# Two-block transformer layer on one core: order of the value units, the odd probabilities and the last gate's tanh

## The chip, the core and the metric

The kernel runs on one core of a Trainium2 chip. A core has TensorE (PE, matmuls into PSUM), VectorE (DVE), ScalarE (ACT), GpSimd (POOL) and SyncE (SP, which here only issues DMAs). The engines run side by side, each through its own list of instructions in order, and wait for one another on semaphores. The metric is the time of one execution on the device, in microseconds.

## The reference, cut to what matters

The reference is two blocks one after the other, on one sequence of 256 tokens and 1024 channels. The change touches only the second, and of it only the part ahead of the experts:

```python
h = rms_norm_2(x, norm1_g[l])
proj = h @ w_in[l]
q, ckv, qi, ki, wi, u, v, ga, gb = jnp.split(proj, splits, axis=-1)
...
q_lat = jnp.einsum('bthd,rhd->bthr', q, w_uk[l])
o_lat = sparse_attention(q_lat, q_idx, w_idx, c_kv, ki, rel_bias)
o_a = jnp.einsum('bthr,rhd->bthd', o_lat, w_uv[l]).reshape(B, T, ATTN_WIDTH)
y_a = o_a @ w_proj_a[l]
y_b = chunked_gmlp(u, v, ln_v_g[l], ln_v_b[l], w_spatial[l], b_spatial[l]) @ w_proj_b[l]
merged = jax.nn.sigmoid(ga) * y_a + jax.nn.sigmoid(gb) * y_b
x = x + merged @ w_out[l]
h2 = rms_norm_2(x, norm2_g[l]).reshape(B * T, D)
y = hier_moe(h2, ...)
```

In `sparse_attention` an index score (queries `qi`, keys `ki`, relu, weighted by `wi`) picks 64 keys for each token; the attention's softmax runs over these, in the latent space `c_kv`. `chunked_gmlp` takes the gelu of `u` and `v`, a layer norm of `v`, mixes the tokens of each chunk of 128 by `w_spatial`, and multiplies by `u`. `hier_moe` is 32 experts, of which each token uses two.

## The kernel before

Everything is float32. A product is made of three matmuls: weights and activations are each split into a high part (`w_hi`, `xT_hi`) and a low part (`w_lo`, `xT_lo`), and `mm3` (L1790 to L1794) adds low by high, high by low and high by high.

The projection of the second block runs in **units** of 256 columns, `w` = 0 to 16. For each unit SyncE loads 1 MB of weights into one of four `raw` slots, ScalarE copies the high part (`hi2`, the activation at L737, possible once TensorE is done with unit `w - 2`), VectorE subtracts to get the low part (`split2`, L1154), and TensorE multiplies, 48 matmuls in two halves, into one of three PSUM banks. In unit `w`'s turn ScalarE and VectorE make the halves of unit `w + 2`. Then ScalarE evacuates the bank of unit `w`. The order of the units stands in a table (L80): `W_QI` 0 and 1 are index queries, `W_K` 2 the keys, `W_Q` 3 and 4 the queries, `W_V` 5 and 6 the gating values v, `W_U` 8 and 9 the gating u, the rest are gates. Columns of w_in_2 are loaded to match.

What depends on the results is woven into the units, by hand, at fixed numbers. On each engine a function `small(w, half)` holds the pieces for half a unit; TensorE runs `small(w, 0)` between the halves of unit `w` and `small(w, 1)` behind them.

- `X_IX` = 4: eight index scores in units 4 to 7 (TensorE L2103, relu on ScalarE L959, weighted sums on VectorE L1465 and L1467). They need the turned keys, which ScalarE copies at the end of its turn 3 (L1015 and L1016).
- `TOP_AT`: VectorE finds the top keys in six parts, at the end of its turns 5, 6, 7 (first 128 tokens) and 9, 10, 11 (the others), by MAX8 and MATCH_REPLACE. The last part of each gives the mask that GpSimd adds to the bias of the scores (L698).
- `GELU_AT`: a gelu unit is evacuated by a square and a copy (L1001, L1002), VectorE's polynomial (L1501, after its split), ScalarE's tanh (L1004), VectorE's product (L1518, after top keys and layer norm if there are any).
- `X_LNV` = 8: in this turn VectorE takes the layer norm's statistics of the value half (L1505 to L1512), behind its split; a turn later ScalarE normalises (L1020), and then GpSimd multiplies by the gain and adds the bias (L688, L690).
- `X_QL` = 8: the queries go to the latent space (L2113).
- `X_SP` = 10: behind unit 10, TensorE mixes the tokens (L2166, waits for GpSimd), and VectorE multiplies by u (L1525). `X_YB` = 11: behind units 11 and 12 the result is turned (L2175), ScalarE takes its high part and VectorE, as the last piece of turns 11 and 12, its low part (`yb_lo`, L1530). The second turning waits for the first `yb_lo`, and the first output matmul of the attention (L473) for the second, since all use one PSUM bank.
- `X_S` = 11: eight attention tasks, two a unit, in units 11 to 14. VectorE adds the bias and takes the maximum (L1481, L1482), ScalarE the exponential (L973), VectorE normalises (`probabilities`, L1452 and L1453), TensorE turns the result two half-units after the scores (L454), then values and output. Before, `small` normalises task s - 1 right ahead of the scores of task s, so that the odd ones come in the turn after their own.

At the end of the units ScalarE's turn 16 holds the high half of unit 18, then the tanh of the last gate (L1007), for which the first unit of the projection (17) waits (`ev2`). Then come the projections, `w_out`, the router and the experts, whose weights (96 MB) stream through a ring of seven tiles that are refilled as TensorE frees them.

Of the kernel before, what the change touches and what calls it, by code (L numbers as in the profile page):

```python
# [58 lines left out]
UCOLS = 2048  # L59
# [19 lines left out]
G2 = LAYERS * UNITS  # L79
W_QI, W_K, W_Q, W_V, W_U, W_PB, W_PA, W_OUT, W_R = 0, 2, 3, 5, 8, 17, 19, 21, 25  # L80
GELU_AT = (W_V, W_V + 1, W_U, W_U + 1)
# [14 lines left out]

X_IX, X_QL, X_LNV, X_SP, X_YB, X_S = 4, 8, 8, 10, 11, 11

# [24 lines left out]
def build(nc, t, out):  # L123
    ctx = ExitStack()
    with ctx:
# [376 lines left out]
        def _(sp):  # L502
# [79 lines left out]
            col_of.update({w: O_GA + 256 * g for g, w in enumerate(GATE_AT)})  # L582
            for w in range(W_Q, W_PB):
                load2(w, w2[:, :, col_of[w]:col_of[w] + 256], KC, 256)
# [138 lines left out]
        def _(act):  # L723
# [252 lines left out]
            for w in range(W_PB):  # L976
                small(w, 0)
                exponentials(w, 0)
                small(w, 1)
                hi2(G2 + w + 2, W_COLS.get(w + 2, UCOLS))  # L980
                exponentials(w, 1)
# [3 lines left out]
                if w == W_K:  # L985
# [6 lines left out]
                    nc.scalar.activation(wi[:], rows[:, :, P + HD:K_COLS], ACT.Copy, scale=IDX_SCALE).then_inc(ev2, 1)  # L992
                elif w < W_Q:
                    nc.scalar.activation(qiT[:, 2 * (w - W_QI):2 * (w - W_QI) + 2, :], two, ACT.Copy).then_inc(ev2, 1)
                elif w < W_V:
                    nc.scalar.activation(q2T[:, 2 * (w - W_Q):2 * (w - W_Q) + 2, :], two, ACT.Copy).then_inc(ev2, 1)
                elif w in GELU_AT:
                    n = GELU_AT.index(w)
                    if n >= 1:
                        act.wait_ge(gel_out, n)  # L1000
                    nc.scalar.activation(gel_s, bank, ACT.Square)  # L1001
                    nc.scalar.activation(gel_x, bank, ACT.Copy, scale=0.5).then_inc(ev2, 1)  # L1002
                    act.wait_ge(gel_poly, n + 1)
                    nc.scalar.activation(gel_s, gel_s, ACT.Tanh, scale=2.0 * GELU_C * 0.044715).then_inc(gel_th, 1)  # L1004
                else:
                    g = 2 * GATE_AT.index(w)
                    nc.scalar.activation(gT[:, g:g + 2, :], two, ACT.Tanh, scale=0.5).then_inc(ev2, 1)  # L1007
# [14 lines left out]
                if w in (X_YB, X_YB + 1):  # L1022
                    r = w - X_YB
                    act.wait_ge(ybT_done, r + 1)
                    nc.scalar.activation(br_hi[:, 1, 2 * r:2 * r + 2, :], ps[:, TB, :].rearrange("p (c t) -> p c t", c=2), ACT.Copy).then_inc(yb_hi, 1)
            for w in range(W_PB, W_OUT):
                hi2(G2 + w + 2, W_COLS.get(w + 2, UCOLS))
                if w >= W_PA:
                    j = w - W_PA
                    act.wait_ge(proj_a, j + 1)  # L1030
                    nc.scalar.activation(xT_hi[:, 4 * j:4 * j + 4, :], gT[:, 4 * j:4 * j + 4, :], ACT.Copy, scale=0.5).then_inc(pm_hi, 1)
# [86 lines left out]
        def _(dve):  # L1118
# [278 lines left out]
            def split2(u, n=UCOLS, i=None):  # L1397
                split(0, u, n, None if i is None else i * 12)
# [56 lines left out]
            def small(w, half):  # L1455
# [15 lines left out]
                s = latent_task(w, half)  # L1471
                if s is not None and s >= 1:
                    probabilities(s - 1)
                if s is not None:
# [7 lines left out]
                    nc.vector.tensor_reduce(nm2[:, s % 4, :], e, AX.X, ALU.max, negate=True).then_inc(s2_max, 1)  # L1482
                if (w, half) == (X_S + 4, 0):
                    probabilities(7)

            for w in range(W_PB):
# [9 lines left out]
                small(w, 1)  # L1496
                split2(G2 + w + 2, W_COLS.get(w + 2, UCOLS))
                if w in GELU_AT:
                    n = GELU_AT.index(w)
# [922 lines left out]
```

## Time and profile before

| | us |
|---|---|
| median of 3 runs | 1373.38 |
| lowest, highest | 1372.72, 1373.8 |
| the profiled execution | 1373.0 |
| its span | 1371.2 |
| TensorE busy | 1290.9 (94%) |
| VectorE busy | 905.2 (66%) |
| ScalarE busy | 586.7 (43%) |
| GpSimd busy | 59.8 (4%) |

The profile is of one execution. Times in it count from the start of the span. A timeline lists the instructions of an engine with their start and length; a number in brackets is the idle time ahead of one and what ended it. An instruction's length covers its whole way through the engine, so that the next one can start a little before its end; a step from start to start is the better measure of cost. A view of stretches gives the busy time of each engine, and the clock that was granted to TensorE, as a share of its full 2.4 GHz. The first block ends at about 913 us, the units of the second run from 922 to 1066, the experts from 1134.

### The profile page before, as it was taken

The page shows a single profiled execution, that of the slowest core. Times are in us where ns is not written, and L with a number is a line of the kernel's source. Part 1 is how long each engine was busy: PE and PEld are TensorE (multiplying, and loading weights), DVE is VectorE, ACT ScalarE, POOL GpSimd, SP SyncE. Part 2 cuts the span into 40 slices and gives each one's busy share as a digit, 9 for nine tenths or more (in the row PEclk, how much of TensorE's full clock was granted, in tenths as well). Part 3 has the DMA queues.
Part 4 walks back from the last instruction along what each step waited for, and adds up shares of the span by engine and source line. Part 5 has one row for each costly group of instructions (what it writes and reads, how often), then busy time and mean ns, then how long its engine had stood idle before and what let it go on. Part 6 is the DMA issues. An engine that isn't in the chain of part 4 may idle for free.

```text
span 1371.2 us, 21689 instructions
## 1 busy us (share of the span) xinstructions
PE 1290.9 (94%) x8713; PEld 1093.8 (80%) x8713; DVE 905.2 (66%) x1464; ACT 586.7 (43%) x911; POOL 59.8 (4%) x84
## 2 busy tenths in 40 slices
PE   7999999999999899999998999969979979999996
PEld 6999999788888799989987888859879866555553
DVE  3999877875555789997687555584885672223223
ACT  3345675434444334566544444444535343111111
POOL 1000000000000000000000000020043000011000
PEclk9999999999999999999999999989989989999998
DMA  9754435465555456443456555555535586999994
GB/s 282 244 196 152 156 93 155 153 215 184 188 193 198 128 184 218 137 154 101 148 183 207 192 184 184 184 172 158 155 111 187 205 303 257 419 420 421 420 421 191
DMA packets 172583, 289.70 MB, mean 211 GB/s; under 512 B 10388, under 2 KB 143140, under 8 KB 160204
## 3 DMA queue, kind: packets, MB, share of 16 engines
q1 hardware_dynamic: 169580, 281.55, 58.6%
q0 software_dynamic: 2752, 6.82, 1.7%
q8 instruction: 62, 1.02, 0.3%
q14 instruction: 29, 0.24, 0.0%
q10 hardware_dynamic: 160, 0.08, 0.0%
HBM read 287.36 MB, written 3.16 MB: 212 GB/s over the span
## 4 chain that ended last, share of the span: by engine, by line
PE 61%; DVE 25%; ACT 5%; DMA 5%; issue 3%; POOL 0%; SPq 0%; DVEq 0%; ACTq 0%; POOLq 0%
PE ps L1792 11%; PE ps L1794 10%; PE ps L1793 10%; DVE w_lo L1154 8%; PE ps L1843 8%; PE ps L2289 7%; DVE cvh L1277 5%; ACT w_hi L737 4%; PE ps L1845 4%; PE ps L2321 3%; DMA raw<-in_w_up 2%; DMA w_exp<-in_w_up 2%; PE ps L2332 2%; DVE nm L1234 1%; DVE gT L1194 1%
## 5 line engine op out<-in xcount | busy, mean ns | idle before, releaser
L1154 DVE TENSOR_TENSOR w_lo<-raw,w_hi 128x2048 fp32r<-128x2048 f32 (+1 forms) x165 | 369.6, 2240 | 147.4 <-ACT w_hi L737 147.2
L737 ACT ACTIVATE w_hi<-raw 128x2048 fp32r<-128x2048 f32 (+1 forms) x165 | 307.4, 1863 | 233.1 <-PE ps L1794 218.4
L1792 PE MATMUL ps<-xT_both,w_lo 128*128 128x256 f32 x680 | 198.1, 291 | 0.0
L1793 PE MATMUL ps<-xT_both,w_hi 128*128 128x256 f32 x680 | 193.3, 284 | 0.0
L1794 PE MATMUL ps<-xT_both,w_hi 128*128 128x256 f32 x680 | 193.0, 284 | 0.0
L1843 PE MATMUL ps<-xT_both,w_hi 128*128 128x512 f32 x496 | 176.0, 400 | 0.0
L1792 PE MATMUL ps<-w_hi,xT_both 128*128 128x256 f32 (+2 forms) x536 | 161.9, 302 | 1.9 <-DVE w_lo L1154 1.7
L1793 PE MATMUL ps<-w_lo,xT_both 128*128 128x256 f32 (+2 forms) x536 | 159.1, 297 | 0.0
L1794 PE MATMUL ps<-w_hi,xT_both 128*128 128x256 f32 (+2 forms) x536 | 159.1, 297 | 0.0
L1792 PEld LDWEIGHTS ps<-xT_both,w_lo 128*128 128x128 f32 x680 | 131.4, 193 | 3.0 <-issue 2.7
L1793 PEld LDWEIGHTS ps<-xT_both,w_hi 128*128 128x128 f32 x680 | 131.3, 193 | 0.2
L1794 PEld LDWEIGHTS ps<-xT_both,w_hi 128*128 128x128 f32 x680 | 131.1, 193 | 0.0
L1845 PE MATMUL ps<-xT_both,w_lo 128*128 128x256 f32 x434 | 121.6, 280 | 0.0
L1792 PEld LDWEIGHTS ps<-w_hi,xT_both 128*128 128x128 f32 x536 | 102.4, 191 | 8.4 <-issue 2.9
L1843 PEld LDWEIGHTS ps<-xT_both,w_hi 128*128 128x128 f32 x496 | 90.8, 188 | 22.3 <-issue 5.3
L1794 PEld LDWEIGHTS ps<-w_hi,xT_both 128*128 128x128 f32 x536 | 102.3, 191 | 2.9
L1793 PEld LDWEIGHTS ps<-w_lo,xT_both 128*128 128x128 f32 x536 | 102.4, 191 | 2.6
L1277 DVE SCALAR_TENSOR_TENSOR cvh<-cvh,prm 128x256 f32<-128x256 f32 x240 | 98.3, 479 | 0.1
L1726 DVE TENSOR_TENSOR xT_both<-ps,xT_both 128x512 fp32r<-128x512 f32 x32 | 22.1, 692 | 113.5 <-ACT xT_both L1106 113.5
L1792 PE MATMUL ps<-w_hi,br_lo 128*128 128x512 f32 x240 | 93.7, 391 | 0.3 <-DVE br_lo L1353 0.3
L1794 PE MATMUL ps<-w_hi,br_hi 128*128 128x512 f32 x240 | 93.4, 389 | 0.0
L1793 PE MATMUL ps<-w_lo,br_hi 128*128 128x512 f32 x240 | 93.4, 389 | 0.0
(410 smaller groups left out, 2264.6 us busy)
## 6 DMA issues: line engine op xcount, KB each, us to landing
raw<-in_w_in SPq DMA_DIRECT2D x72, 1024.0 KB, 5.1
raw<-in_w_ff SPq DMA_DIRECT2D x64, 1024.0 KB, 5.3
raw<-in_w_down SPq DMA_DIRECT2D x10, 1024.0 KB, 16.0
raw<-in_w_up SPq DMA_DIRECT2D x10, 1024.0 KB, 17.5
w_exp<-in_w_down SPq DMA_DIRECT2D x10, 1024.0 KB, 17.6
raw<-in_w_o SPq DMA_DIRECT2D x8, 1024.0 KB, 4.9
w_exp<-in_w_gate SPq DMA_DIRECT2D x8, 1024.0 KB, 16.9
raw<-in_w_gate SPq DMA_DIRECT2D x8, 1024.0 KB, 17.7
```

Source lines behind the costliest of these rows:

```text
L737: nc.scalar.activation(split_of(u)[0][:, 0:n], raw[:, u % RAW, 0:n], ACT.Copy).then_inc(hi_done, 1)
L1154: nc.vector.tensor_tensor(split_of(u)[1][:, 0:n], raw[:, u % RAW, 0:n], split_of(u)[0][:, 0:n].bitcast(F32), ALU.subtract).then_inc(split_ ...
L1277: nc.vector.scalar_tensor_tensor(out=cv[:, c, :], in0=hpad[:, c, k:k + T], scalar=w, in1=cv[:, c, :], op0=ALU.mult, op1=ALU.add).then_inc( ...
L1726: nc.vector.tensor_tensor(y_lo[h], ps[:, Y_BANKS[h], :], y_hi[h].bitcast(F32), ALU.subtract).then_inc(y_lod[h], 1)
L1792: nc.tensor.matmul(out_, left[1], right[0], start=start, stop=False)
L1793: nc.tensor.matmul(out_, left[0], right[1], start=False, stop=False)
L1794: return nc.tensor.matmul(out_, left[0], right[0], start=False, stop=stop)
L1843: last = nc.tensor.matmul(both, w_c[0][:, k, :], xT_both[:, k].rearrange("p i t -> p (i t)"), start=k == 0, stop=k == KC - 1)
L1845: nc.tensor.matmul(high, w_c[1][:, k, :], xT_hi[:, k, :], start=False, stop=False)
L2289: last = nc.tensor.matmul(gate_up(r, p)[s, kind * T:(kind + 1) * T], x, duos[duo_slot(r, d)][e][:, k * T:(k + 1) * T], start=k == 0, stop= ...
L2321: last = nc.tensor.matmul(ps[s, Y_BANKS[h], :], heT[:, c, s], duos[duo_slot(r, d)][e][:, c * D + h * BANK:c * D + (h + 1) * BANK], start=c ...
L2332: last = nc.tensor.matmul(ps[:, ACC + 2 * a + h, :], place[p % PLACES][:, a, :], y, start=p == 0 and k == 0, stop=p == PAIRS - 1 and k == 1)
```

## The change

Three things, all in the second block:

1. The table of units: the value units are now 3 and 4, the query units 5 and 6, and `X_LNV` is 5. The loads and the evacuations follow. `X_QL`, `X_IX`, `TOP_AT` and `X_SP` stay.
2. VectorE's `small` normalises task s - 1 only in the second half of a unit, which are the even tasks; the odd ones are normalised behind the split of their own turn, ahead of the top keys.
3. On ScalarE the high half of unit 18 comes behind the last gate's tanh.

```diff
--- before.py
+++ after.py
@@ -77,7 +77,7 @@
 O_Q, O_KV, O_QI, O_KI, O_WI, O_U, O_V, O_GA, O_GB = (int(c) for c in np.cumsum((0, 512, 128, 512, 64, 8, 512, 512, 1024)))
 
 G2 = LAYERS * UNITS
-W_QI, W_K, W_Q, W_V, W_U, W_PB, W_PA, W_OUT, W_R = 0, 2, 3, 5, 8, 17, 19, 21, 25
+W_QI, W_K, W_V, W_Q, W_U, W_PB, W_PA, W_OUT, W_R = 0, 2, 3, 5, 8, 17, 19, 21, 25
 GELU_AT = (W_V, W_V + 1, W_U, W_U + 1)
 GATE_AT = (7, 10, 11, 12, 13, 14, 15, 16)
 TOP_AT = {5: (0, 0), 6: (0, 1), 7: (0, 2), 9: (1, 0), 10: (1, 1), 11: (1, 2)}
@@ -94,7 +94,7 @@
 PLACES = 3
 PROJ_BANKS = ((5, 6), (7, 4))
 
-X_IX, X_QL, X_LNV, X_SP, X_YB, X_S = 4, 8, 8, 10, 11, 11
+X_IX, X_QL, X_LNV, X_SP, X_YB, X_S = 4, 8, 5, 10, 11, 11
 
 
 def raw_inc(u):
@@ -580,7 +580,7 @@
             col_of = {W_Q + j: O_Q + 256 * j for j in range(2)}
             col_of.update({w: o for w, o in zip(GELU_AT, (O_V, O_V + 256, O_U, O_U + 256))})
             col_of.update({w: O_GA + 256 * g for g, w in enumerate(GATE_AT)})
-            for w in range(W_Q, W_PB):
+            for w in range(W_K + 1, W_PB):
                 load2(w, w2[:, :, col_of[w]:col_of[w] + 256], KC, 256)
             for w0, name in ((W_PB, "w_proj_b_2"), (W_PA, "w_proj_a_2")):
                 for j in range(2):
@@ -977,7 +977,8 @@
                 small(w, 0)
                 exponentials(w, 0)
                 small(w, 1)
-                hi2(G2 + w + 2, W_COLS.get(w + 2, UCOLS))
+                if w < W_PB - 1:
+                    hi2(G2 + w + 2, W_COLS.get(w + 2, UCOLS))
                 exponentials(w, 1)
                 bank = ps[:, UB + w % 3, :]
                 two = bank.rearrange("p (c t) -> p c t", c=2)
@@ -990,9 +991,9 @@
                     for i in range(2):
                         nc.scalar.activation(ki2[:, :, i, :], rows[:, :, P:P + HD], ACT.Copy)
                     nc.scalar.activation(wi[:], rows[:, :, P + HD:K_COLS], ACT.Copy, scale=IDX_SCALE).then_inc(ev2, 1)
-                elif w < W_Q:
+                elif w in (W_QI, W_QI + 1):
                     nc.scalar.activation(qiT[:, 2 * (w - W_QI):2 * (w - W_QI) + 2, :], two, ACT.Copy).then_inc(ev2, 1)
-                elif w < W_V:
+                elif w in (W_Q, W_Q + 1):
                     nc.scalar.activation(q2T[:, 2 * (w - W_Q):2 * (w - W_Q) + 2, :], two, ACT.Copy).then_inc(ev2, 1)
                 elif w in GELU_AT:
                     n = GELU_AT.index(w)
@@ -1023,6 +1024,7 @@
                     r = w - X_YB
                     act.wait_ge(ybT_done, r + 1)
                     nc.scalar.activation(br_hi[:, 1, 2 * r:2 * r + 2, :], ps[:, TB, :].rearrange("p (c t) -> p c t", c=2), ACT.Copy).then_inc(yb_hi, 1)
+            hi2(G2 + W_PB + 1)
             for w in range(W_PB, W_OUT):
                 hi2(G2 + w + 2, W_COLS.get(w + 2, UCOLS))
                 if w >= W_PA:
@@ -1469,7 +1471,7 @@
                 for kind, s in latent_steps(w, half):
                     latent_dve(dve, kind, s)
                 s = latent_task(w, half)
-                if s is not None and s >= 1:
+                if s is not None and half == 1:
                     probabilities(s - 1)
                 if s is not None:
                     nk = P * (s // 4 + 1)
@@ -1480,8 +1482,6 @@
                         dve.wait_ge(t2_done, s - 3)
                     then(nc.vector.tensor_tensor(e, ps[:, s % 2, :].rearrange("p (i k) -> p i k", i=2)[:, :, 0:nk], bias_t[:, s % 2, :, 0:nk], ALU.add))
                     nc.vector.tensor_reduce(nm2[:, s % 4, :], e, AX.X, ALU.max, negate=True).then_inc(s2_max, 1)
-                if (w, half) == (X_S + 4, 0):
-                    probabilities(7)
 
             for w in range(W_PB):
                 if w == W_K + 1:
@@ -1495,6 +1495,8 @@
                 small(w, 0)
                 small(w, 1)
                 split2(G2 + w + 2, W_COLS.get(w + 2, UCOLS))
+                if latent_task(w, 1) is not None:
+                    probabilities(latent_task(w, 1))
                 if w in GELU_AT:
                     n = GELU_AT.index(w)
                     dve.wait_ge(ev2, w + 1)

```

In the changed kernel lines move by one (from ScalarE's gate on) or two (VectorE and after).

**ScalarE, from the high half made in turn 3 on.** `gT` is the gelu's working space, `cvh` the turned keys, `qkT` the queries. Before:

```order
L737 ACTIVATE w_hi<-raw 128x2048
L996 ACTIVATE qkT<-ps 128x512
L1015 ACTIVATE cvh<-ps 128x256
L1016 ACTIVATE cvh<-ps 128x256
L959 ACTIVATE wide<-ps 128x2x128 x2
```

After:

```order
L737 ACTIVATE w_hi<-raw 128x2048
L1002 ACTIVATE gT<-ps 128x512
L1003 ACTIVATE gT<-ps 128x512
L1005 ACTIVATE gT<-gT 128x512
L1016 ACTIVATE cvh<-ps 128x256
L1017 ACTIVATE cvh<-ps 128x256
L959 ACTIVATE wide<-ps 128x2x128 x2
```

One copy ahead of the turned keys has become three activations, the last of which waits for VectorE.

**VectorE, turn 5 and the start of turn 6.** The L1424 group is the first top keys, L1465 to L1468 the index sums, L1154 the split. Before (ahead of it the split of turn 5):

```order
L1501 SCALAR_TENSOR_TENSOR gT<-gT 128x512
L1424 TENSOR_TENSOR wide<-wide,mask 128x128
L1425 MAX nw<-wide 128x8
...
L1518 SCALAR_TENSOR_TENSOR vv<-gT 128x2x256
L1465 TENSOR_SCALAR wide<-wide,wi 128x256
L1467 SCALAR_TENSOR_TENSOR wide<-wide,wi 128x256
L1468 MEMSET nw 128x1
L1467 SCALAR_TENSOR_TENSOR wide<-wide,wi 128x256 x2
L1468 MEMSET nw 128x1
L1154 TENSOR_TENSOR w_lo<-raw,w_hi 128x2048
```

After, from the split of turn 5 (L1156), layer norm (L1507 to L1514), top keys (L1426 on), index sums, split of turn 6:

```order
L1156 TENSOR_TENSOR w_lo<-raw,w_hi 128x2048
L1507 BN_STATS st<-vv 128x6 x2
...
L1514 SCALAR_TENSOR_TENSOR nmr<-mv,nw 128x2
L1426 TENSOR_TENSOR wide<-wide,mask 128x128
L1427 MAX nw<-wide 128x8
...
L1467 TENSOR_SCALAR wide<-wide,wi 128x256
L1469 SCALAR_TENSOR_TENSOR wide<-wide,wi 128x256
L1470 MEMSET nw 128x1
L1469 SCALAR_TENSOR_TENSOR wide<-wide,wi 128x256 x2
L1470 MEMSET nw 128x1
L1156 TENSOR_TENSOR w_lo<-raw,w_hi 128x2048
```

The layer norm now stands ahead of the top keys of turn 5, and index sums and the split of unit 8's weights follow them; the gelu's polynomial and product are gone from here.

**VectorE, turn 11, from its split to the next score.** L1452 and L1453 normalise task 1, L1432 begins the last top keys, L1443 ends them, L1530 is `yb_lo`. Before:

```order
L1154 TENSOR_TENSOR w_lo<-raw,w_hi 128x2048
L1432 MAX nw<-cvh 128x8
...
L1443 TENSOR_TENSOR cvh<-cvh,mask 128x128
L1530 TENSOR_TENSOR br_lo<-ps,br_hi 128x512
L1452 RECIPROCAL rs<-rs 128x2
L1453 TENSOR_TENSOR qkT<-qkT,rs 128x2x128
```

After:

```order
L1156 TENSOR_TENSOR w_lo<-raw,w_hi 128x2048
L1454 RECIPROCAL rs<-rs 128x2
L1455 TENSOR_TENSOR qkT<-qkT,rs 128x2x128
L1434 MAX nw<-cvh 128x8
...
L1445 TENSOR_TENSOR cvh<-cvh,mask 128x128
L1532 TENSOR_TENSOR br_lo<-ps,br_hi 128x512
```

The two normalising instructions have moved from behind the top keys and `yb_lo` to ahead of them.

**ScalarE, turn 16.** L1007 is the last gate's tanh, L737 the high halves. Before:

```order
L489 ACTIVATE cvh<-ps 128x256
L492 ACTIVATE br_hi<-ps 128x128 x2
L737 ACTIVATE w_hi<-raw 128x2048
L1007 ACTIVATE gT<-ps 128x512
L737 ACTIVATE w_hi<-raw 128x2048 x3
```

After:

```order
L489 ACTIVATE cvh<-ps 128x256
L492 ACTIVATE br_hi<-ps 128x128 x2
L1008 ACTIVATE gT<-ps 128x512
L737 ACTIVATE w_hi<-raw 128x2048 x4
```

The tanh now stands ahead of the high half, which joins the three that follow.

## Rows read from the trace of the kernel before

**Rows 1.** Timeline of TensorE: start, length (us), engine, line, tiles, [idle before, releaser].
```profile
1004.40 3.78 PE L2166 MATMUL ps<-vv,rot 128*128 128x128 f32 x16 [6.75 <-POOL vv L690]
...
1024.81 0.44 PE L454 MATMUL ps<-ident,qkT 128*128 128x128 f32 x2 [2.69 <-DVE qkT L1453]
...
1031.86 0.44 PE L473 MATMUL ps<-cvh,gT 128*64 128x128 f32 x4 [0.23 <-DVE br_lo L1530]
...
1068.93 0.36 PE L1792 MATMUL ps<-br_hi,w_lo 128*128 128x256 f32 x1 [2.71 <-ACT gT L1007]
```

**Rows 2.** Timelines of VectorE, ScalarE, TensorE: unit 3's end, a polynomial, a tanh.
```profile
948.48 2.29 DVE L1154 TENSOR_TENSOR w_lo<-raw,w_hi 128x2048 fp32r<-128x2048 f32 x1 [0.78 <-ACT w_hi L737]
...
949.09 0.39 ACT L1016 ACTIVATE cvh<-ps 128x256 f32<-128x256 f32 x1
...
951.22 0.49 PE L2103 MATMUL ps<-cvh,qkT 64*128 64x128 f32 x4
...
966.60 0.68 DVE L1501 SCALAR_TENSOR_TENSOR gT<-gT 128x512 f32<-128x512 f32 x1
...
967.32 0.63 ACT L1004 ACTIVATE gT<-gT 128x512 f32<-128x512 f32 x1 [1.99 <-DVE gT L1501]
```

**Rows 3.** Timelines of VectorE (top keys, index sums, layer norm) and TensorE (unit 8's start).
```profile
967.21 0.28 DVE L1424 TENSOR_TENSOR wide<-wide,mask 128x128 f32<-128x128 f32 x1
...
970.40 0.69 DVE L1518 SCALAR_TENSOR_TENSOR vv<-gT 128x512 f32<-128x512 f32 x1
...
971.01 0.35 DVE L1465 TENSOR_SCALAR wide<-wide,wi 128x256 f32<-128x256 f32 x1
...
972.97 2.29 DVE L1154 TENSOR_TENSOR w_lo<-raw,w_hi 128x2048 fp32r<-128x2048 f32 x1
...
989.60 1.28 DVE L1505 BATCH_NORM_STATS2 st<-vv 128x6 f32<-128x512 f32 x2
...
993.45 0.68 DVE L1518 SCALAR_TENSOR_TENSOR vv<-gT 128x512 f32<-128x512 f32 x1
...
976.84 0.39 PE L1792 MATMUL ps<-w_hi,xT_both 128*128 128x256 f32 x1
```

**Rows 4.** Timelines of ScalarE, GpSimd and VectorE around the two multiplies.
```profile
971.86 0.58 ACT L1001 ACTIVATE gT<-ps 128x512 f32<-128x512 f32 x1
...
997.66 1.50 ACT L1020 ACTIVATE vv<-vv,nmr,nw 128x512 f32<-128x512 f32 x2
...
999.25 2.35 POOL L688 TENSOR_TENSOR vv<-vv,wide 128x1024 f32<-128x1024 f32 x1 [72.18 <-ACT vv L1020]
...
1001.68 2.67 POOL L690 TENSOR_TENSOR vv<-vv,wide 128x1024 f32<-128x1024 f32 x1
...
1000.28 0.43 DVE L1429 MAX8 nw<-cvh 128x8 f32<-128x256 f32 x1
...
1002.08 4.42 DVE L1154 TENSOR_TENSOR w_lo<-raw,w_hi 128x2048 fp32r<-128x2048 f32 x1
```

**Rows 5.** Stretches, TensorE alone: from:to, length, PE busy, granted clock, DMA share, GB/s.
```profile
1009.00:1010.00 1.00, 1.00 (x10) 0.93 1.07 382
...
1029.00:1030.00 1.00, 1.00 (x8) 0.69 0.00 0
```

**Rows 6.** Timeline of VectorE from the last products on.
```profile
1012.01 0.42 DVE L1481 TENSOR_TENSOR qkT<-ps,wide 128x256 f32<-128x256 f32 x1 [0.48 <-PE ps L2126]
...
1014.03 0.93 DVE L1453 TENSOR_TENSOR qkT<-qkT,rs 128x256 f32<-128x256 f32 x1
...
1015.32 0.42 DVE L1481 TENSOR_TENSOR qkT<-ps,wide 128x256 f32<-128x256 f32 x1 [0.36 <-PE ps L2126]
...
1016.89 2.60 DVE L1154 TENSOR_TENSOR w_lo<-raw,w_hi 128x2048 fp32r<-128x2048 f32 x1 [0.69 <-ACT w_hi L737]
```

**Rows 7.** Timeline of ScalarE, the weight half ahead of the last tanh.
```profile
1066.44 1.90 ACT L737 ACTIVATE w_hi<-raw 128x2048 fp32r<-128x2048 f32 x1
```

**Rows 8.** Stretches, all engines: busy us of each, PEclk, DMA share, GB/s.
```profile
1200.00:1250.00 50.00, 50.00 (x344) 27.82 (x341) 13.79 (x27) 7.56 (x16) 4.73 (x8) 1.00 1.01 421
```

## The prediction

> **What bounds the kernel now.** I read the timeline of the tensor engine first, and in it the rows that carry an idle time. Between the end of the first block and the experts it waits long at four places only [rows 1]: 6.75 us for GpSimd's second multiply on the value half (ahead of the spatial matmuls), 2.69 us for the odd probabilities of task 1, 0.23 us for VectorE's low half of the second turned branch (`yb_lo`), 2.71 us for the tanh of the last gate. The change aims at the first, second and fourth. The third looks harmless, and is what to watch: it says that at 1031.86 VectorE, not TensorE, set the pace. From the row of the last products (L1525) on, VectorE's own chain (scores, exponentials, splits, top keys) runs up to that point almost without a pause [rows 6]. What TensorE gains ahead of 1031.86 is therefore worth only what VectorE's chain gains with it.
>
> The experts follow everything. There the DMA engines are full (share 1.01, 421 GB/s, [rows 8]) and refill a ring of tiles that TensorE frees, so whatever TensorE's start there moves by, the end moves by, one for one.
>
> The sum is made against the profiled execution, 1373.0 us (span 1371.2 and 1.8 around it), which lies 0.4 under the median of the three runs, 1373.38. About 0.2% (2.7 us) is what a measurement of this kernel can tell from no change.
>
> **Part 1: value units at 3 and 4.** The same matmuls, the same splits; what moves is who waits.
>
> (a) Unit 3's evacuation on ScalarE was one copy; now it is square, copy, a wait for VectorE's polynomial, tanh, and only then the copies of the turned keys, for which the first index score waits. VectorE can give the polynomial after the split that starts at 948.48, which takes 2.2 us until the next instruction can start: 950.7. From polynomial to tanh is 0.72 us (966.60 to 967.32), the tanh takes 0.54 to its successor (its row lists 0.63 of busy time), so the key copies start at 951.95 and end 0.65 later at 952.60, where they ended at 949.48; with 0.1 us of handing over TensorE goes on at 952.70. It came for the first index score at 951.22 [rows 2]. Cost **+1.5 us**, and TensorE is the pace from there to unit 7.
>
> (b) The layer norm's statistics leave unit 8's turn of VectorE, where it had room, for unit 5's, right ahead of the first top keys. At unit 5 VectorE was through with its split at 966.60 [rows 2], now at 968.08. Behind that in program order: layer norm 3.85 us (989.60 to 993.45), top keys 3.19 (967.21 to 970.40), the two index sums of unit 6 1.96 (971.01 to 972.97), then the split of unit 8's weights, 2.29. That gives 979.37. TensorE began unit 8 at 976.84 and would be ready for it at 978.3 [rows 3]. So even undisturbed it waits 1.1 us.
>
> (c) It is not undisturbed. GpSimd's two multiplies come as soon as ScalarE has normalised. ScalarE began unit 5's evacuation at 971.86 for the split behind it; the same place, now at unit 6, is 973.3, plus 0.5 for the copy of the queries, plus 1.5 for the two normalising activations: 975.3. GpSimd runs from 975.4, and at 975.1 VectorE has just left the top keys for the index sums. In the trace the split that met the second multiply took 4.42 us instead of 2.29, while a MAX8 inside the first took its 0.43 [rows 4]. So top keys pass, splits and sums with two operands wait, about 2.1 us for each multiply (4.42 less 2.29). SyncE's load of unit 12 follows the same split and so comes 7 us late too; it has three units' turns as cover. Four index-sum instructions and the split stand there, so that both multiplies find one to hold: 979.37 plus 4.2 is 983.6. TensorE waits **5.3 us** and starts unit 8 6.8 us later than before (1.5 of it is (a)).
>
> The page Advanced Engine Details and Errata of the Trainium skill (VectorE Performance Modes) says that GpSimd's instructions and VectorE's two-port ones block each other, and VectorE: DVE Perf Modes (Why tensor_tensor can't do 2×_2P) that a tensor_tensor is never one of these. By these two together the split would run free and at most the first index sum be held. The trace disagrees: the held split is a tensor_tensor with both operands in SBUF. By the pages the time would be that of rival B below, by the row that of this sum.
>
> (d) After such a wait the clock of TensorE is granted low. After the 6.75 us wait it was at its lower level, 1.2 GHz, for 4.7 us (1004.4 to 1009.1), and after the 2.69 us wait for 3.3 us (1026.4 to 1029.7), though that one came 1.6 us after the restart [rows 1, 5]. Half of such a time is lost: 2.35 and 1.6 at most. The wait here lies between; I take 2.2 as nearer to the long one. TensorE and all that hangs on its unit ends is then **9.0 us** late at unit 9, and with it the split of unit 11, from which VectorE works without a pause to the last products.
>
> (e) What is won: the 4.42 us split becomes 2.29, **-2.1**. The 6.75 us wait goes, but only for TensorE: it arrives 3 us early at the turning of the branch and waits there for the same products. The last products end 9.0 - 2.1 = +6.9 late.
>
> **Part 2: odd probabilities.** No instruction is added; each odd normalisation stands one place earlier. The chain from the last products to `yb_lo` of unit 12 changes so: two idle times of VectorE fall away because TensorE and ScalarE are ready early, 0.48 and 0.69, -1.2, and a wait of 0.36 for TensorE's scores, -0.3. Task 1's stood in this chain before too, so moving it is free, save that it now meets GpSimd's bias add (as task 0's did: 0.93 against the 0.42 of an add of the same size, [rows 6]), +0.5. Task 3's stood behind `yb_lo` and now stands ahead of it: some 0.6 for its two instructions (0.93 less the 0.5, and a small reciprocal) and up to 1.0 us behind GpSimd's 512-wide add (half of what the 1024-wide multiply holds), +1.6. Sum **+0.6**. Tasks 5 and 7 are free: VectorE idles there. The 2.69 us wait goes, but TensorE then waits longer at `yb_lo`. It resumes 6.9 + 0.6 = **7.5 us** late at the place of 1031.86.
>
> (f) That wait is again 3 us or more, so a low clock behind it: as after the 2.69 us wait, +1.6 at most. But before, half of unit 13 was slow too and ended at this very point, so part is no news; between 0 and 2.4 I take **+1.6**, by the row of the 2.69 us wait.
>
> **Part 3: the last tanh.** Its row starts 0.1 behind the end of a weight half that starts at 1066.44 and takes 1.90; now the tanh starts at 1066.44. TensorE waits 0.9 instead of 2.71: **-1.8**. The weight half, 0.6 later, has unit 17's 5.8 us of matmuls as cover; without that cover it would cost 0.6 [rows 1, 7].
>
> Sum: 7.5 + 1.6 - 1.8 = +7.3, 1373.0 + 7.3 = **1380.3 us**. Bounds of the clock terms: (d) 1.6 to 2.4, (f) 0 to 2.4, so 1378.1 to 1381.3. If only one of the two multiplies holds VectorE up, 2.1 less and a shorter slow clock (0.6 less), 1377.6.
>
> **Rivals.**
> A. The forecast, slower. For it: four instructions in program order, each with its row.
> B. GpSimd doesn't hold the index sums and the split (they fall beside top keys, or pass). Then TensorE waits 1.1 at unit 8 with no clock lost: 1.5 + 1.1 = +2.6, -2.1, +0.6, -1.8, clock 0 to +1.6: -0.7 to +0.9, 1372.3 to 1373.9, no change. It decides with the start of the multiplies: if they begin before 973, top keys cover most of them.
> C. Faster: VectorE keeps up. If the tanh and the layer norm cost no wait at units 4 and 8 (because ScalarE reaches the key copies in time and some row above is shorter there), what is left is -2.1 + 0.6 - 1.8 = -3.3, and 0 to 1.6 of clock: 1369.7 to 1371.3. It needs the split of unit 8 before 976.9, 2.5 us under the undisturbed chain of (b). That the three waits just vanish (6.75 + 2.69 + 1.8 = 11.2 us less, 1361.8) I exclude: two of them stand ahead of a wait for VectorE.
>
> **How the numbers follow.** A 0.62 (1378.1 to 1381.3 by its clock bounds), one multiply only 0.10 (about 1377.6), B 0.18, C 0.10. C gives faster 0.10 (its upper end, 1371.3, is just not faster; its chance is kept whole because a shorter clock loss is as likely there); the rest of B and a little of the single multiply give same 0.20; slower 0.70. The range takes in B and A's bounds and the upper half of C, 1370.0 to 1383.0; above A it leaves 1.7 us for a third low clock, behind the wait at the first turning of the branch, which the sum has at nothing because VectorE's chain covers it.
>
> **What would show it.** In the timeline after: an idle of 1.5 us ahead of the first index score (A, B); ahead of unit 8 one of 5 us released by VectorE's split (A), of 1 us (B), none (C); no wait ahead of the spatial matmuls; instead waits of about 3 us at both turnings of the branch and at the first output matmul, released by L1525's and L1530's successors; the tanh wait at 0.9. VectorE's index-sum rows at unit 6 with 2 us more each would confirm the block. I am wrong if TensorE's wait ahead of unit 8 is under 2 us, or if the waits at the turnings are short.

## The result and the profile after

| | us |
|---|---|
| changed kernel, median of 5 runs | 1378.41 (1376.98 to 1379.61) |
| before, on the same chip, median of 5 | 1373.38 (1372.16 to 1373.80) |
| ratio, 95% interval | 1.0036 (1.0024 to 1.0047) |
| profiled execution, its span | 1379.22, 1377.4 |
| TensorE, VectorE, GpSimd busy | 1292.9, 908.2, 57.2 |

Slower by 5.0 us, as forecast: 1380.3 was 1.9 too high. The profiled execution is 6.2 above that of before, of which the sum had said 7.3. The work is the same (TensorE's busy time differs by 2 us); what differs is who waits. The timeline of TensorE in the changed kernel, the rows with an idle time between unit 3 and the last gate, in the order of [rows 1] (start, length, engine, line, tiles, [idle before, releaser]):

```profile
947.48 0.33 PE L2159 MATMUL ps<-ident,cvh 128*128 128x128 f32 x1 [1.32 <-DVE cvh L1493]
952.36 0.49 PE L2105 MATMUL ps<-cvh,qkT 64*128 64x128 f32 x4 [1.35 <-ACT cvh L1017]
983.15 0.58 PE L1794 MATMUL ps<-w_hi,xT_both 128*128 128x256 f32 x1 [5.09 <-DVE w_lo L1156]
1017.84 0.66 PE L2177 MATMUL ps<-ident,vv 128*128 128x128 f32 x4 [3.16 <-DVE vv L1527]
1029.37 0.63 PE L2177 MATMUL ps<-ident,vv 128*128 128x128 f32 x4 [1.87 <-DVE br_lo L1532]
1037.74 0.69 PE L473 MATMUL ps<-cvh,gT 128*64 128x128 f32 x4 [4.21 <-DVE br_lo L1532]
1075.38 0.36 PE L1794 MATMUL ps<-br_hi,w_lo 128*128 128x256 f32 x1 [0.91 <-ACT gT L1008]
```

The three long waits of before are gone or short: none ahead of the spatial matmuls (6.75), none for the probabilities (2.69), 0.91 for the tanh (2.71) [rows 1]. The first row stood before too. Of the others the last is what is left of the 2.71; the five between (1.35, 5.09, 3.16, 1.87, 4.21) are new or longer, and VectorE releases four of them. The one of 5.09 ahead of unit 8 is the new thing. VectorE and GpSimd just ahead of it (timelines of both, same columns):

```profile
974.84 0.35 DVE L1467 TENSOR_SCALAR wide<-wide,wi 128x256 f32<-128x256 f32 x1
975.23 5.02 DVE L1469 SCALAR_TENSOR_TENSOR wide<-wide,wi 128x256 f32<-128x256 f32 x2
980.28 0.48 DVE L1469 SCALAR_TENSOR_TENSOR wide<-wide,wi 128x256 f32<-128x256 f32 x1
980.81 2.29 DVE L1156 TENSOR_TENSOR w_lo<-raw,w_hi 128x2048 fp32r<-128x2048 f32 x1
...
975.09 2.40 POOL L688 TENSOR_TENSOR vv<-vv,wide 128x1024 f32<-128x1024 f32 x1 [48.28 <-ACT vv L1021]
977.57 2.40 POOL L690 TENSOR_TENSOR vv<-vv,wide 128x1024 f32<-128x1024 f32 x1
```

Two index-sum instructions take 5.02 us together; they end at 980.25, 0.3 after GpSimd's second pass (977.57 + 2.40 = 979.97). The split behind them, which TensorE waits for, is undisturbed at 2.29 but starts at 980.81, where before it started at 972.97 [rows 3].

To compare executions I count from the matmul of unit 3 at 947.48 (before: 947.76), the last place that the change doesn't touch; it comes between 945.87 (part 1 alone) and 948.32 (parts 2 and 3) in the profiled executions, though what runs up to there is the same work in all of them. The table gives the distance from there to the first output matmul (L473, before at 1031.86) and to the one that waits for the last gate (before at 1068.93), in the profiled execution of each kernel, and the medians of the timed runs against those of before on the same chip. All experiments, which follow, are in it.

| kernel | wait ahead of unit 8 | to L473 | to last gate | against before | median (before) |
|---|---|---|---|---|---|
| before | 0 | 84.10 | 121.17 | | |
| changed | 5.09 | 90.26 | 127.90 | +6.73 | 1378.41 (1373.38) |
| part 1 alone | 5.08 | 88.24 | 125.32 | +4.15 | 1377.92 (1373.53) |
| part 2 alone | 0 | 85.37 | 122.44 | +1.27 | 1376.23 (1373.53) |
| part 3 alone | 0 | 83.75 | 119.03 | -2.14 | 1370.06 (1373.53) |
| parts 2 and 3 | 0 | 85.38 | 120.65 | -0.52 | 1371.24 (1373.82) |
| changed, key copies first | 5.09 | 87.95 | 124.77 | +3.60 | 1374.74 (1373.53) |
| changed, top keys later | 0 | 82.99 | 118.27 | -2.90 | 1371.49 (1373.91) |
| changed, tiny multiplies | 1.09 | 84.22 | 121.06 | -0.11 | 1372.49 (1373.91) |
| changed, task 3 late | 5.09 | 88.50 | 126.58 | +5.41 | 1378.10 (1373.91) |
| the three edits together | 0 | 80.16 | 115.43 | -5.74 | 1368.37 (1373.91) |
| the same without part 2 | 0 | 79.83 | 115.10 | -6.07 | 1367.52 (1373.82) |

What one execution's distance and what the medians say of an edit differ by up to 2.4 us (key copies first: +3.60 and +1.2). Part of that goes with the granted clock, as the section on what was not expected shows.

### The profile page after: what moved, and what is told of

Its sections match the earlier page's. It is cut to its first block, busy times and chain, and to the rows that moved or that the text cites. A ratio compares the mean times of both kernels' runs of the same rounds, so it can differ in the third digit from the quotient of the medians.

```text
span 1377.4 us, 21689 instructions
## 1 busy us (share of the span) xinstructions
PE 1292.9 (94%) x8713; PEld 1095.4 (80%) x8713; DVE 908.2 (66%) x1464; ACT 586.7 (43%) x911; POOL 57.2 (4%) x84
## 3 DMA queue, kind: packets, MB, share of 16 engines
HBM read 287.36 MB, written 3.16 MB: 211 GB/s over the span
## 4 chain that ended last, share of the span: by engine, by line
PE 61%; DVE 27%; ACT 5%; DMA 3%; issue 3%; SPq 1%; DVEq 0%; ACTq 0%
PE ps L1794 10%; PE ps L1796 10%; PE ps L1795 10%; DVE w_lo L1156 9%; PE ps L1845 8%; PE ps L2291 7%; DVE cvh L1279 5%; ACT w_hi L737 4%; PE ps L1847 3%; PE ps L2323 3%; DMA raw<-in_w_up 2%; PE ps L2334 2%; DVE nm L1236 1%; DVE gT L1196 1%; DVE x_nat L1202 1%
## 5 line engine op out<-in xcount | busy, mean ns | idle before, releaser
L1156 DVE TENSOR_TENSOR w_lo<-raw,w_hi 128x2048 fp32r<-128x2048 f32 (+1 forms) x165 | 367.1, 2225 | 152.2 <-ACT w_hi L737 152.1
L737 ACT ACTIVATE w_hi<-raw 128x2048 fp32r<-128x2048 f32 (+1 forms) x165 | 307.4, 1863 | 230.3 <-PE ps L1796 215.4
```

What stands on the lines that cost most here:

```text
L737: nc.scalar.activation(split_of(u)[0][:, 0:n], raw[:, u % RAW, 0:n], ACT.Copy).then_inc(hi_done, 1)
L1156: nc.vector.tensor_tensor(split_of(u)[1][:, 0:n], raw[:, u % RAW, 0:n], split_of(u)[0][:, 0:n].bitcast(F32), ALU.subtract).then_inc(split_ ...
```

## Experiments

### The three parts, each by itself

Each is the diff's own lines of that part (`W_V`, `W_Q`, `X_LNV` and the loads; `probabilities`; `hi2` of unit 18), with the others as before.

**Part 1 alone.** 

> Part 1 alone (value units at 3 and 4, layer norm in turn 5); odd probabilities and last tanh as before. The theory of the prediction: part 1 carries the whole loss. The wait of 5.1 us ahead of unit 8 stays as in the changed kernel (which hangs on nothing of parts 2 and 3), the wait for the last tanh is 2.7 again instead of 0.9 (+1.8), and what part 2 gave back in the chain to the first output matmul (measured -0.3) is missing. About 1378.4 + 1.8 + 0.3 = 1380.5, +7 over before. Rival (part 2 is what costs, through the normalisation ahead of yb_lo): then this kernel stands at or under before, 1371 to 1374, with no wait ahead of unit 8.

Measured: 1377.92, ratio 1.0037 (1.0024 to 1.0050), 4.4 slower. The wait ahead of unit 8 is 5.08, so it belongs to part 1 and needs nothing of the others. The rival falls. But the expectation of +7 was too high: the first output matmul is only 4.14 late (88.24 - 84.10), 2.0 less than in the changed kernel. So part 2 takes 2.0 us there, where I had taken it to give back 0.3. TensorE's wait and VectorE's rows with part 1 alone:

```profile
981.55 0.58 PE L1792 MATMUL ps<-w_hi,xT_both 128*128 128x256 f32 x1 [5.08 <-DVE w_lo L1154]
...
1015.69 0.41 DVE L1481 TENSOR_TENSOR qkT<-ps,wide 128x256 f32<-128x256 f32 x1
...
1018.55 0.41 DVE L1481 TENSOR_TENSOR qkT<-ps,wide 128x256 f32<-128x256 f32 x1
...
1019.33 2.28 DVE L1154 TENSOR_TENSOR w_lo<-raw,w_hi 128x2048 fp32r<-128x2048 f32 x1
```

The three idle times of [rows 6] (0.48, 0.36, 0.69) are gone and the split takes 2.28, not 2.60, without part 2. Once part 1 has made VectorE late, TensorE and ScalarE are ready for it. I had booked this gain to part 2.

**Part 2 alone.** 

> Odd probabilities alone, on the kernel before. The theory: the 2.69 us wait ahead of 1024.81 goes, and TensorE waits instead for yb_lo at the place of 1031.86, because VectorE's chain from the last products to yb_lo is hardly shorter. The 0.48 of idle time goes, the normalisation of task 3 now stands ahead of yb_lo (+1.3 by its row in the changed kernel): -1 to +1.5 us, 1372.4 to 1374.9, that is no change. Rival (the waits of TensorE simply add up): the 2.69 us and the low clock behind it go, 1373.4 - 2.7 - 1.6 = 1369.1.

Measured: 1376.23, ratio 1.0020 (1.0009 to 1.0030), slower by 2.7. The rival, in which the waits of TensorE add up to a gain, is out, and my own range was too low by 1.3. In the trace the 2.69 is gone and TensorE waits for `br_lo` twice:

```profile
1024.20 0.72 PE L2175 MATMUL ps<-ident,vv 128*128 128x128 f32 x4 [1.99 <-DVE br_lo L1530]
1032.56 0.44 PE L473 MATMUL ps<-cvh,gT 128*64 128x128 f32 x4 [2.68 <-DVE br_lo L1530]
1069.63 0.55 PE L1792 MATMUL ps<-br_hi,w_lo 128*128 128x256 f32 x1 [2.71 <-ACT gT L1007]
```

By distance it loses 1.27, within what was expected. The rest came later, behind the last gate's wait: from there to the end of the span are 305.4 us, before 302.3. Parts 2 and 3 together, below, are the test of that.

**Part 3 alone.** 

> Last tanh ahead of the weight half alone, on the kernel before. The theory: TensorE's wait there falls from 2.71 to 0.9 us, and since nothing behind it waits for another engine, the end moves by the same 1.8: 1373.4 - 1.8 = 1371.6. Rival (the stream of weights sets the end, not TensorE's start): no change, 1373.4, with the wait gone all the same.

Measured: 1370.06, ratio 0.9974 (0.9963 to 0.9984), 3.5 faster. The wait is 0.91 as forecast, and the end follows TensorE's start: the rival falls. The gain is nearly twice the 1.8 of the wait, and 1.5 more than expected. Why is not shown. In the profiled pair 2.1 of the 3.9 us of span come behind the matmul that I count from (2.14 at the last gate); the other 1.8 stand ahead of it, where the kernels do the same (granted clock of the first 50 us 1.00, before 0.93).

**Parts 2 and 3.** 

> Parts 2 and 3 on the kernel before, part 1 left out. Part 2 alone came out at 1376.2 with runs from 1373.3 to 1379.5; its profiled run shows the granted clock at 0.71 from 1070 to 1080, behind the 2.71 us wait for the last tanh, and its slow runs are those of low mean clock (0.973 against 0.978). Theory: that low clock is what part 2 alone paid beyond its chain (+1.3 at the first output matmul), and part 3 shortens the wait ahead of it to 0.9. So 1373.5 + 1.3 - 1.8 = 1373.0, no run with a mean clock under 0.975, and a spread of 3 us or less. Rival (the low clock comes from the waits at the turnings, not from the one for the tanh): 1376.2 - 1.8 = 1374.4, and the spread stays at 6 us.

Measured: 1371.24, ratio 0.9983 (0.9974 to 0.9992), 11 runs from 1370.5 to 1373.0. That is 5.0 under part 2 alone, for a wait shortened by 1.8. Mean clocks run from 0.977 to 0.981, with part 2 alone from 0.973 to 0.979. Stretches behind the last gate's wait, with part 2 alone, then with parts 2 and 3 (from:to, length, busy us of PE, PEld, DVE, ACT, POOL, granted clock, DMA share, GB/s):

```profile
1070.00:1072.00 2.00, 2.00 (x11) 2.00 (x11) 1.37 (x1) 0.00 (x0) 0.00 (x0) 0.50 1.04 438
1072.00:1074.00 2.00, 2.00 (x11) 2.00 (x11) 0.00 (x0) 0.00 (x0) 0.00 (x0) 0.50 0.97 406
1074.00:1076.00 2.00, 2.00 (x12) 2.00 (x11) 0.00 (x0) 0.00 (x0) 0.00 (x0) 0.55 1.02 416
```

```profile
1070.00:1072.00 2.00, 2.00 (x19) 2.00 (x18) 1.29 (x1) 0.67 (x1) 0.00 (x0) 1.00 0.92 385
1072.00:1074.00 2.00, 2.00 (x19) 2.00 (x18) 1.00 (x1) 0.00 (x0) 0.00 (x0) 1.00 1.01 422
```

At 0.50 TensorE gets 11 matmuls through in 2 us, at 1.00 19. From the last gate to the end the profiled execution takes 302.2 us, with part 2 alone 305.4: the low clock cost 3.1, more than the 2.71 us wait ahead of it. Of the theory the spread was met (2.5, and no clock under 0.975); the time fell 1.8 further than its 1373.0. The rival (1374.4, spread 6) falls. So the 2.71 us wait for the tanh is followed by a low clock in some executions (in the profiled ones of part 1 and of part 2 alone, not in that of before), and with part 3 neither profiled execution shows it. Why it follows in some only isn't settled.

### What holds VectorE ahead of unit 8

**Tiny multiplies.** The output is incomplete: most of the layer norm's gain and bias is left out.

```diff
-    nc.gpsimd.tensor_tensor(vg, vg, bc(lnv_g, 1, TT), ALU.mult)
+    nc.gpsimd.tensor_tensor(vg[:, :, 0:2], vg[:, :, 0:2], bc(lnv_g[:, 0:2], 1, TT), ALU.mult)
...
-    nc.gpsimd.tensor_tensor(vg, vg, bc(lnv_b, 1, TT), ALU.add)
+    nc.gpsimd.tensor_tensor(vg[:, :, 0:2], vg[:, :, 0:2], bc(lnv_b[:, 0:2], 1, TT), ALU.add)
```

> The changed kernel with GpSimd's multiply and add of the layer norm done on 2 of the 128 columns of each tile, so that most of the gain and bias of the value half is left out. All other instructions stand. The theory (GpSimd's two instructions hold VectorE's index sums): the two index-sum instructions that took 5.02 us together take about 2 again, the wait ahead of unit 8 falls from 5.1 to 1.5 or so, with a shorter low clock: 4 to 5.5 us less, 1373 to 1374.5. Rival (VectorE is late by its own queue, and the sums are slow by themselves): the sums keep their 5 us and the time stays at 1378.4.

Measured: 1372.49, ratio 0.9996 (0.9987 to 1.0005); 1.4 under its own before. The same instructions of VectorE at the same place:

```profile
975.55 1.01 DVE L1469 SCALAR_TENSOR_TENSOR wide<-wide,wi 128x256 f32<-128x256 f32 x2
...
977.12 2.29 DVE L1156 TENSOR_TENSOR w_lo<-raw,w_hi 128x2048 fp32r<-128x2048 f32 x1
...
975.39 0.20 POOL L688 TENSOR_TENSOR vv<-vv,wide 128x4 f32<-128x4 f32 x1 [47.51 <-ACT vv L1021]
...
979.46 0.39 PE L1794 MATMUL ps<-w_hi,xT_both 128*128 128x256 f32 x1 [1.09 <-DVE w_lo L1156]
```

5.02 us became 1.01, and TensorE's wait 5.09 became 1.09: exactly the 1.1 that step (b) gives for an undisturbed VectorE. The 4.0 us of difference are GpSimd's doing. To the first output matmul the kernel gains 6.04 (90.26 - 84.22), 4.0 of wait and 2.0 of clock behind it. The time fell a little further than expected, the rival is out.

**Top keys later.**

```diff
-TOP_AT = {5: (0, 0), 6: (0, 1), 7: (0, 2), 9: (1, 0), 10: (1, 1), 11: (1, 2)}
+TOP_AT = {6: (0, 0), 7: (0, 1), 8: (0, 2), 9: (1, 0), 10: (1, 1), 11: (1, 2)}
```

> The changed kernel with the first half of the top keys in turns 6, 7 and 8 of VectorE instead of 5, 6 and 7; nothing else is moved. The theory (VectorE's queue in turn 5 is the loss, its 3.2 us of top keys and 4.2 us of holding by GpSimd's two multiplies): the index sums of unit 6 stand right behind the layer norm, at 971.6 instead of 974.8; the first multiply at 975.1 falls beside the split of unit 8's weights or beside top keys. The wait ahead of unit 8 falls from 5.1 to between 0 and 1, and its low clock goes: 5 to 7 us less, 1371.5 to 1373.5, at best 1370. Rival (only the place of the layer norm counts, GpSimd's share is small): top keys moved away give 3.2 at most, 1375.2 or more.

Measured: 1371.49, ratio 0.9987 (0.9978 to 0.9996), at the lower end of the expectation; that is 0.13% under the kernel before, within the 0.2% that counts as no change. No wait is left ahead of unit 8:

```profile
972.34 1.01 DVE L1469 SCALAR_TENSOR_TENSOR wide<-wide,wi 128x256 f32<-128x256 f32 x2
...
973.91 2.29 DVE L1156 TENSOR_TENSOR w_lo<-raw,w_hi 128x2048 fp32r<-128x2048 f32 x1
...
976.12 2.48 DVE L1426 TENSOR_TENSOR wide<-wide,mask 128x128 f32<-128x128 f32 x1
978.63 0.29 DVE L1427 MAX8 nw<-wide 128x8 f32<-128x128 f32 x1
...
975.45 3.00 POOL L688 TENSOR_TENSOR vv<-vv,wide 128x1024 f32<-128x1024 f32 x1 [48.31 <-ACT vv L1021]
978.53 2.41 POOL L690 TENSOR_TENSOR vv<-vv,wide 128x1024 f32<-128x1024 f32 x1
```

The split of unit 8 is through before GpSimd can get at it, and it is GpSimd that waits: its first pass takes 3.00, not 2.40. Then the masking, 128 columns that take 0.28 elsewhere, takes 2.48 beside that pass, and MAX8 and MATCH_REPLACE run beside the second pass at their usual 0.29 and 0.28. One of two passes still finds an instruction to hold, but behind the split, not ahead of it.

### Key copies first

```diff
+                if w == W_K + 1:
+                    act.wait_ge(lateT_done, KV_T)
+                    nc.scalar.activation(ckvT, ps[:, TB, 0:T], ACT.Copy)
+                    nc.scalar.activation(kiT, ps[:, TB, T:2 * T], ACT.Copy).then_inc(lateT_c, 1)
                 bank = ps[:, UB + w % 3, :]
```

The same four lines are taken out behind the evacuation.

> The changed kernel with ScalarE's copies of the turned keys ahead of the evacuation of value unit 3, not behind it. The theory: the wait of 1.35 us ahead of the first index score goes. VectorE's chain from unit 5's split is then the bound: that split starts up to 1.3 us earlier, and layer norm, top keys, index sums and the split of unit 8 follow it. TensorE's wait ahead of unit 8 stays near 5 us, as VectorE and GpSimd start earlier by the same. End about -1.3: 1377.1. Rival (VectorE's chain to unit 8 hangs on something other than TensorE's unit 5): the wait of 1.35 goes and the one ahead of unit 8 grows by as much, 1378.4.

Measured: 1374.74, ratio 1.0008 (0.9999 to 1.0016). The wait of 1.35 is gone, the one ahead of unit 8 is 5.09 to the hundredth, as expected: VectorE, ScalarE and GpSimd all start from TensorE's unit 5. So step (a) passes on one for one: unit 8 starts 1.4 earlier. By distance to the last gate the gain is 3.1, and the other 1.7 is clock: the low stretch behind the wait at unit 8 is shorter (from restart to the first turning 33.81 us, changed kernel 34.69), and so is that behind the 4.2 us wait (from L473 to the last gate 36.82, changed 37.64). The median fell 3.7 us where 1.3 was expected, and the kernel can't be told from the one before.

### Task 3's normalisation late

```diff
-                if latent_task(w, 1) is not None:
+                if latent_task(w, 1) not in (None, 3):
                     probabilities(latent_task(w, 1))
...
                                             br_hi[:, 1, 2 * r:2 * r + 2, :].bitcast(F32), ALU.subtract).then_inc(yb_lo, 1)
+                if latent_task(w, 1) == 3:
+                    probabilities(3)
```

> The changed kernel with the normalisation of task 3 behind yb_lo of unit 12's turn, where the kernel before had it, the other odd ones as changed. The theory: yb_lo is the end of VectorE's chain that TensorE waits for (4.21 us at 1037.74), so it comes 1.3 us earlier, and the end with it: 1377.1. Rival (the chain was bound by the transposes or by ScalarE's high half there): no change, 1378.4.

Measured: 1378.10, ratio 1.0035 (1.0022 to 1.0047). In the trace the wait at L473 falls from 4.21 to 2.81, by 1.4 where 1.3 was expected, and L473 comes 1.76 earlier (88.50 against 90.26). Behind it the low clock takes 0.4 of that back (from L473 to the last gate 38.08 us instead of 37.64), which leaves 1.3 at the last gate. The medians show less: 0.3, or 0.8 against their own befores (+4.2 and +5.0), with intervals that overlap. Of the theory the place is shown, the gain in time isn't.

### The edits together

> The three edits together on the changed kernel: key copies ahead of the evacuation of unit 3, top keys one turn later, task 3's normalisation behind yb_lo. The theory (each takes away one term of the loss): 1.3 + 5 to 7 + 1.3 less, 1368.8 to 1371, faster than the kernel before by 2 to 4 us. Rival (a second chain stands right behind each): no more than the best of the three alone, 1371.5 to 1373.5.

Measured: 1368.37, ratio 0.9963 (0.9949 to 0.9976): 5.5 faster than the kernel before. That is 0.4 under the expected 1368.8 to 1371, the rival falls, and the single terms nearly add: the distance to the last gate falls by 12.5, and 3.1, 9.6 and 1.3 by the edits alone make 14.0. Of the difference 0.9 is clock behind unit 8, which the key copies and the top keys each win back alone, and 0.4 is clock behind L473. Last question: does part 2 pay here?

> The fastest kernel so far (key copies ahead of the evacuation of unit 3, top keys one turn later, last tanh first) with the odd probabilities all put back where the kernel before had them. Theory: what part 2 takes out of TensorE's waits comes back at yb_lo, and with task 3's normalisation behind yb_lo it costs and gives nothing: 1368.4 within 0.5; TensorE waits some 2.6 us for the probabilities of task 1 and 0.3 at the first output matmul, in place of 3.4 and 1.3. Rival (with part 1's block gone part 2 does pay): 1.5 us or more above, 1369.9 or more.

Measured: 1367.52, ratio 0.9952 (0.9938 to 0.9965), the fastest version; the intervals of the two overlap. TensorE's waits with and without part 2 (first three rows with it):

```profile
1009.84 0.66 PE L2179 MATMUL ps<-ident,vv 128*128 128x128 f32 x4 [3.16 <-DVE vv L1527]
1021.38 0.63 PE L2179 MATMUL ps<-ident,vv 128*128 128x128 f32 x4 [3.38 <-DVE br_lo L1532]
1028.35 0.44 PE L473 MATMUL ps<-cvh,gT 128*64 128x128 f32 x4 [1.30 <-DVE br_lo L1532]
```

```profile
1009.26 1.12 PE L2177 MATMUL ps<-ident,vv 128*128 128x128 f32 x4 [3.16 <-DVE vv L1527]
1020.38 0.44 PE L454 MATMUL ps<-ident,qkT 128*128 128x128 f32 x2 [2.71 <-DVE qkT L1455]
1027.44 0.44 PE L473 MATMUL ps<-cvh,gT 128*64 128x128 f32 x4 [1.76 <-DVE br_lo L1532]
```

7.8 us of waits with it, 7.6 without. The median is 0.9 under the expected 1368.4 (within 0.5), and the wait at L473 is 1.76, not 0.3; the rival (1.5 us or more above) falls. With task 3's normalisation left behind `yb_lo`, as in both kernels here, part 2 only chooses where TensorE waits for VectorE. Where the whole of part 2 cost 1.3 and 2.0 us, task 3's stood ahead of `yb_lo`; by the run that moved it back it is worth 1.8 at L473.

Part 3 alone gave 3.5 us and this kernel gives 6.3. By the difference, part 1 with its two edits is worth some 2.8 us; no run compares the two directly.

## Why the prediction was right, step by step

The direction and the main mechanism (a second chain on VectorE, lengthened by GpSimd, ahead of unit 8) were right. The closeness of the total is in part luck, since part 2 was put 1.0 too high and (f) 0.8 too low.

- **(a)** 1.5 forecast, 1.35 measured; right, and shown by the key copies.
- **(b), (c)** Wait ahead of unit 8: 5.3 forecast, 5.09 measured, 1.09 without GpSimd's part (1.1 forecast). The multiplies began at 975.09 (975.4 forecast). The start of unit 8 moved by 6.6 from the common origin (6.8 forecast). The choice between case A and rival B, which turned on whether top keys cover GpSimd, was decided as the sum had it. One detail differs: both passes were spent on the first index sums, none on the split.
- **(d)** 2.2 forecast, about 2.0 measured (tiny multiplies: 34.69 against 32.66 from restart to the turning). With the copies first it was 1.2, for the same wait of 5.09: a size that one execution doesn't fix.
- **(e)** The split of unit 12 takes 2.28 instead of 4.42. The last products start, and end, 6.54 late in the changed kernel (the start 68.15 against 61.61 from the origin); +6.9 was forecast.
- **Part 2** is the step that failed in its terms. +0.6 was the sum for the chain to L473; measured from the last products it is -0.4, so L473 came 6.2 late, not 7.5. Of the terms, idle times gone gave 1.8 (1.5 forecast), task 1's normalisation cost 0.34 (0.5), task 3's 1.41 (1.6), and a split shorter by 0.3 was not in the sum. And the first of these belongs to part 1: by itself part 2 costs 1.3 on the kernel before and 2.0 on top of part 1. The rule that TensorE's gain counts only as far as VectorE's chain gains was right. Waits of about 3 us were forecast at both turnings and at L473; they are 3.16, 1.87 and 4.21. The second is short, which the prediction had named as a sign against it. It is short because TensorE did its work ahead of it slowly: from turning to turning it is 11.53 us in the changed kernel and 11.55 with the top keys later, but there, at a granted clock of 1.00 between them, the wait is 3.36, and here the clock was 0.50 from 1020 to 1022.
- **(f)** 1.6 forecast, 2.4 measured in the changed kernel: from L473 to the last gate 37.64 against 37.07, while the wait for the tanh inside it is 1.8 shorter. The row of clock there:

```profile
1038.00:1042.00 4.00, 4.00 (x17) 3.31 (x15) 1.67 (x3) 0.63 (x3) 0.00 (x0) 0.50 0.53 204
```

- **Part 3** -1.8 forecast and measured in the wait. In time it was -3.5 alone, and the rest is not explained. The low clock that stands behind the 2.71 us wait in some executions, which the sum didn't have, is not enough: among runs with the same mean clock, 0.978, part 3 alone took 1368.8 to 1370.2 us (3 runs) and before, on the same chip, 1372.4 to 1374.4 (11).
- **The start.** "At four places only" was misread: the kernel before also waits 10.48 us at 918.49, and 4.50 at 1125.12 and 2.11 at 1128.48 ahead of the experts. They stand in the changed kernel too (10.69, 4.50, 2.12), so the sum didn't need them.

The sum by what was measured: 6.16 + 2.37 - 1.80 = 6.73 at the last gate, less 0.28 at the origin and 0.25 in the experts, is 6.2 for the profiled pair. The medians differ by 5.0. The forecast was 1.1 over the profiled pair (0.4 up to the last products and 1.0 in part 2, less 0.8 in (f), and the 0.5 at the origin and in the experts); the other 1.2 lies between one execution and the median, whose runs spread over 2.6 us.

The rivals describe kernels that were run later. With tiny multiplies TensorE waits 1.09 at unit 8 and the distance to the last gate is 0.1 under before, within rival B's -0.7 to +0.9. With the top keys out of the way VectorE keeps up at unit 8, and the distance falls to 2.9 under before, near the 3.3 that rival C gives ahead of its clock (though the 1.35 at unit 4 still stands there).

## What to carry to other kernels

A step moved to an earlier turn takes its successors on other engines along: here GpSimd's two passes came 24 us earlier, out of a place where they held up one split and into one where they held the index sums with a more urgent split behind them, and the cure was to move other work (the top keys) from ahead of that split, not the step itself. When several waits of TensorE in a row are released by the same engine, removing one of them only lengthens the next; count that engine's chain instead. And a low-clock stretch behind a wait can cost more than the wait (3.1 us behind 2.71 here), in part of the executions only, so compare medians of many runs beside the single trace.

## What was not expected of the hardware

**A held instruction is the one that starts.** Beside GpSimd's 128x1024 passes with two operands, VectorE's scalar_tensor_tensor (two took 5.02 instead of 1.01) and a tensor_tensor of 128 columns (2.48 instead of 0.28) did not get on until the pass ended: each lost 2.0 to 2.2 us, whatever its own length. MAX8 and MATCH_REPLACE passed at 0.29 and 0.28. It goes both ways: a pass that came during a split took 3.00 instead of 2.40. The Trainium skill, in SBUF — State Buffer (Who interferes with whom), says that an instruction of VectorE with two SBUF inputs contends with a GpSimd instruction that reads SBUF, and that whichever comes first blocks the other for its whole length. These rows agree with it in both directions (4.0 us lost by VectorE, 0.6 by GpSimd); the two sections named in the prediction speak of the two-port modes alone, and what I made of them, that the split would run free, these rows contradict.

**The spread goes with the granted clock.** Runs of part 2 alone by their mean clock: 0.973 took 1377.2 to 1379.5 us (4 runs), 0.976 and 0.977 took 1375.5 to 1376.8 (4), 0.978 and 0.979 took 1373.3 to 1374.0 (4). In the same comparison the kernel before has clocks from 0.974 to 0.979, with 1371.1 to 1375.3. The mean clock alone doesn't fix the time: one run of before, compared with parts 2 and 3, shows 0.931 and took 1374.6. The same wait was not followed by the same clock. Behind the tanh's 2.71 us it was 0.50 for nearly 7 us in one profiled execution (part 2 alone) and 1.00 in another (before). At L473 a wait of 2.81 was followed by a loss of 2.8 us, one of 4.21 by 2.4, one of 4.20 by 1.5, one of 2.69 (top keys later) by none, against the 35.3 us that the stretch from L473 to the last gate takes with a wait of 0.91 and the clock at 1.00. What decides it isn't settled by these runs.
